# A new planner table and two changes of order in a hybrid decoder trunk whose token mixing runs beside an expert gather

## The reference

```
h = rmsnorm(x) @ w_in                      # u_a, v_a, val_b, gate_b, q_m and three gates, 1024 each
y_a = gelu(u_a) * (tril(w_s) @ layernorm(gelu(v_a)) + b)    # chunks of 128 tokens, 8 groups
y_b = silu(layernorm(causal_depthwise(val_b * sigmoid(gate_b), 31 taps)))
y_m = softmax(q_m k^T / 16) v              # 4 heads, 256 memory rows
x = x + (sig(g_a)*(y_a@w_o_a) + sig(g_b)*(y_b@w_o_b) + sig(g_m)*(y_m@w_o_m)) @ w_out
q = rmsnorm(x) @ w_q                       # 8 retrieval heads, product keys: two top-16 of 128,
                                           # then the top 16 of their 256 sums
x = x + sum over 8*16 experts of softmax(score) * gelu(xn . u_e) * v_e      # 16384 experts
```

## Time and profile before

| | |
|---|---|
| median of 3 runs | 2350.17 us (2345.11 to 2351.42) |
| profiled execution | 2351.42 us, its span 2348.7 us |
| PE, DVE, ACT, POOL busy | 69%, 67%, 28%, 29% |
| moved by DMA | 906 MB, of it 604 MB by POOL's gathers |

### The profile page before, as it was taken

The page is one execution under the profiler, slowest core; times in us unless marked ns, Lnnn a source line. Parts: engine busy times, 40 slices in busy tenths (PEclk is TensorE's granted clock), DMA queues, the critical chain, the costliest instruction groups (busy, mean ns, idle before and its releaser), DMA issues.

```text
span 2348.7 us, 32536 instructions
## 1 busy us (share of the span) xinstructions
PE 1625.2 (69%) x11468; PEld 1147.6 (49%) x11468; DVE 1584.5 (67%) x4217; ACT 666.4 (28%) x1654; POOL 677.7 (29%) x606
## 2 busy tenths in 40 slices
PE   8999848758898549777777635866899843333333
PEld 7899826527786217555666403743778610000000
DVE  2672258867766567898665556985966667776774
ACT  2112132521142323432131223342123233323221
POOL 0000032313233333232332232221422344444442
PEclk9999969968899759998899756986989965555555
DMA  7586699999899999999999999999989999999996
GB/s 278 178 303 238 249 386 401 418 421 388 355 419 420 420 409 422 421 421 422 421 420 420 421 418 382 394 421 408 370 354 421 420 421 421 418 422 411 417 408 272
DMA packets 127841, 905.98 MB, mean 386 GB/s; under 512 B 16112, under 2 KB 16576, under 8 KB 18368
## 3 DMA queue, kind: packets, MB, share of 16 engines
q0 software_dynamic: 82944, 604.02, 62.3%
q1 hardware_dynamic: 44736, 299.90, 32.2%
HBM read 895.75 MB, written 8.11 MB: 385 GB/s over the span
## 4 chain that ended last, share of the span: by engine, by line
PE 32%; DMA 31%; DVE 22%; ACT 4%; DVEq 4%; issue 4%; POOL 2%; POOLq 0%; SPq 0%; ACTq 0%
DMA uv<-uv_in,idx_u 24%; PE bank L1200 19%; DVE uv L1108 9%; DMA ring<-cache_in 5%; PE bank L1206 5%; PE bank L1574 4%; DVE yB L786 3%; POOL uv L405 2%; DMA ring<-w_in 2%; DVEq L781 1%; DVE x L1129 1%; ACT diag L731 1%; ACT L464 1%; DVE merged L794 1%; DVE yB L797 1%
## 5 line engine op out<-in xcount | busy, mean ns | idle before, releaser
L405 POOL DMA_INDIRECT uv<-uv_in,idx_u x576 | 635.5, 1103 | 1473.2 <-PE bank L1574 1066.8
L1108 DVE CUSTOM_DVE_ANT_0 uv<-uv,xrep 128x1024 f32<-128x1024 f32 x576 | 685.8, 1229 | 241.4 <-DMA uv<-uv_in,idx_u 240.9
L1574 PE MATMUL bank<-uv,diag 128*32 128x512 f32 x2304 | 431.1, 830 | 553.7 <-ACT diag L731 553.7
L1200 PEld LDWEIGHTS bank<-xnT,ring 128*128 128x128 f32 x4096 | 565.4, 206 | 105.1 <-issue 93.0
L1200 PE MATMUL bank<-xnT,ring 128*128 128x128 f32 (+1 forms) x4096 | 593.1, 307 | 6.8 <-DMA ring<-w_in 5.3
L1574 PEld LDWEIGHTS bank<-uv,diag 128*32 128x32 f32 x2304 | 55.2, 125 | 783.1 <-ACT diag L731 719.0
L464 ACT ACTIVATE pick<-pick 128x2 f32<-128x2 f32 (+1 forms) x324 | 69.6, 215 | 1128.9 <-DVE pick L1108 1128.3
L786 DVE SCALAR_TENSOR_TENSOR yB<-ext_p,small,yB 128x128 f32<-128x128 f32 x960 | 280.5, 354 | 20.4 <-issue 0.9
L464 ACT ACT_TABLE_LOAD x145 | 186.0, 1283 | 7.1 <-DMA x<-x_in 4.5
L731 ACT ACTIVATE diag<-gated_fold,pick 128x32 f32<-128x32 f32 x576 | 153.6, 314 | 9.7 <-ACT pick L464 0.3
L1200 PE MATMUL bank<-yMA,ring 128*128 128x128 f32 (+1 forms) x1024 | 136.7, 288 | 0.0
(11 more groups left out here) (161 smaller groups left out, 1481.4 us busy)
## 6 DMA issues: line engine op xcount, KB each, us to landing
ring<-w_in SPq DMA_DIRECT2D x224, 1024.0 KB, 9.8
ring<-cache_in SPq DMA_DIRECT2D x32, 1024.0 KB, 17.2
uv<-uv_in,idx_u POOLq DMA_INDIRECT x576, 17.2
phase<-rows_in SPq DMA_DIRECT2D x4, 1024.0 KB, 17.2
ring<-keys_in SPq DMA_DIRECT2D x4, 1024.0 KB, 10.1
ext_s<-state_in SPq DMA_DIRECT2D x2, 1088.0 KB, 10.4
convs_out<-ext_s SPq DMA_DIRECT2D x2, 1088.0 KB, 19.7
ext_s<-mem_in SPq DMA_DIRECT2D x2, 1024.0 KB, 18.5
```

What stands on the lines that cost most here:

```text
L405: nc.gpsimd.indirect_dma_start(out=uvbuf[2 * b + i], out_offset=None, in_=uv_in, in_offset=bass.IndirectOffsetOnAxis(ap=ids[:, c:c + 1], a ...
L1108: ins = V.tensor_tensor_reduce(out=u, in0=u, in1=xrep[gg % 2][:, :], scale=1.0, scalar=0.0, op0=ALU.mult, op1=ALU.add, accum_out=hid[:, c: ...
L1200: ins = MM(out, w[:, k, P * b:P * (b + 1)], rhs(k), start=k == 0, stop=k == KB - 1)
L1574: ins = MM(vbank[gg % 2][c:c + 32, :], diag[:, t % 4, i], uvbuf[2 * b + i][:, D + 512 * n:D + 512 * (n + 1)], start=first, stop=last)
```

## The change

It has four parts.

1. The planner's costs in `parts`: sk and sv 2 to 2.5; sg 1.5 to 2.5; csum and csq 2.5 to 3; tr2 9 to 12. `TAIL` 11 to 14.
2. The order of dense pieces: before, sg0, ua3, sg1, sg2, mg8, sg3, mg9; after, sg0, ua3, sg1, sg2, sg3, mg8, mg9. It holds in `parts` (and so in the turn of banks) and in PE's generator.
3. DVE's `gated`: the wait for projection and gate and the merge come before `conv(taps)`, not behind it, and the pieces 0, 8 and 16 start at the place of the next piece, not 2 units behind it.
4. For p = 1, ACT does `weigh(2)` (the exponential of head 2) behind `va(0)`, not ahead of it, and DVE does `att_norm(2)` ahead of `att_max(3)`.

```diff
-        out += some("sk", 2, 0, 1, 2) + O(3) + some("sk", 2, 3, 4, 5, 6, 7) + some("pts", 0.8, 0) + some("va", across, 3)
-        out += some("sv", 2, 0, 1) + some("pts", 0.8, 1) + some("sv", 2, 2, 3, 4, 5, 6, 7)
+        out += some("sk", 2.5, 0, 1, 2) + O(3) + some("sk", 2.5, 3, 4, 5, 6, 7) + some("pts", 0.8, 0) + some("va", across, 3)
+        out += some("sv", 2.5, 0, 1) + some("pts", 0.8, 1) + some("sv", 2.5, 2, 3, 4, 5, 6, 7)
...
-    out += some("mg", h, *range(2, 8)) + some("ua", h, 0, 1, 2) + some("sg", 1.5, 0)
-    out += some("ua", h, 3) + some("sg", 1.5, 1, 2) + some("mg", h / 2, 8) + some("sg", 1.5, 3) + some("mg", 3 * h / 2, 9) + [("csum", 2.5)] + some("mg", h, 10, 11, 12) + [("csq", 2.5)]
+    out += some("mg", h, *range(2, 8)) + some("ua", h, 0, 1, 2) + some("sg", 2.5, 0)
+    out += some("ua", h, 3) + some("sg", 2.5, 1, 2, 3) + some("mg", h, 8, 9) + [("csum", 3)] + some("mg", h, 10, 11, 12) + [("csq", 3)]
...
-    out += [("tr2", 9)] + some("wq", h, 0, 1) + some("sc", 1, 0) + some("wq", h, 2, 3) + some("sc", 1, *range(1, STEPS[p]))
+    out += [("tr2", 12)] + some("wq", h, 0, 1) + some("sc", 1, 0) + some("wq", h, 2, 3) + some("sc", 1, *range(1, STEPS[p]))
...
-LEAD, TAIL = 2, 11
+LEAD, TAIL = 2, 14
...
                     yield from turned(1)
-                    weigh(2)
                     yield place["S3"]
                     va(0)
+                    weigh(2)
...
+                    att_norm(2)
                     yield from att_max(3)
-                    att_norm(2)
...
-                        yield place[f"mg{c + 1}"] + 2 if c % 8 == 0 else place[f"mg{c}"]
-                        conv(taps)
+                        yield place[f"mg{c + 1 if c % 8 == 0 else c}"]
                         dve.wait_ge(S["pe_proj"], at("pe_proj", m, c + 1))
...
                             V.tensor_tensor(out, out, gate_c, ALU.add).then_inc(S["mg"], 1)
+                        conv(taps)
...
                 yield from spatial(2)
+                yield from spatial(3)
                 yield place["mg8"]
                 gate(8)
-                yield from spatial(3)
```

## The result

The change made the kernel slower: 2370.53 us (median of 4 runs, 2368.29 to 2372.66) against 2348.96 us for the kernel before beside it, a ratio of 1.0094 with a 95% interval of 1.0081 to 1.0107, or +22 us (+19 to +25). I had forecast 2341 us, range 2331 to 2354. The profiled execution after took 2376.01 us, its span is 2373.5 us, 24.8 us above the span before.

The account below looks back on a forecast made before the run. The prediction took the kernel to be bound by DMA bytes behind the start-up. From 2351.4 us it took 14.6 for two dry places, added 4.7 for a convolution, giving 2341.5, stated as 2341 us, range 2331 to 2354.

Parts of the forecast that it names:

- What bounds the kernel: Behind the start-up, DMA bytes at some 420 GB/s; the share falls short by 29.8 us, in few places.
- The pace and TAIL: More dense work beside each pair leaves PE less margin, 0.7 us instead of 1.0, but costs 0.
- the 13 us that I had called free: DMA's outstanding gathers last long enough that some 13 us between two `values` costs nothing, while 20 us does.
- my rivals: Dry places stay, 2351 (0.25); slower, 2359 (0.13); more than two places, 2333 (0.12); PE full, 2348 to 2351, counted with the first.
- Part 2 with the sg costs: At sg0 to mg9, p = 1: PE's long gap before sg3 goes, -14.6 us; the other end is 0.
- both dry places: Around sg3 in the two p = 1 mixings, 625 to 635 and 1725 to 1740 us: 7.6 and 7.0 us, both to go.
- Part 3: In DVE's gated pieces: piece 0's convolution loses idle time, +4.7 us; merges waiting for tanh cost 0.
- work in store: DMA's outstanding work hides tanh waits of merges in k = 3 and 5 pairs: 0, upper end 4.3 us.
- My slower rival: Merges wait 1.1 us in each of 8 gated pieces, 22 us with the convolution against -14.6: 2359 us; chance 0.13.
- POOL's multiplications: Layer norm of v, beside mg1 to mg4: as many DVE instructions stretched as before, 0, ends -2 and +2 us a portion.
- Part 4: With p = 1, DVE waits 3 us a portion for ACT's later exponential, hidden behind full DMA: 0, at most 6 us.
- The base of the sum: The terms were added to 2351.4 us, the profiled execution of the kernel before.

Follow-up runs that it names:

- e3: Kernel before with only the merge put ahead of the convolution and the 2 units of delay dropped: 2359.05 us, ratio 1.0048.
- e5: Kernel after with POOL's mask of the spatial weights moved earlier, from ua1's place to ua0's: 2351.43 us, 1.0015 of the kernel before.
- e7: Kernel before with only TAIL changed from 11 to 14: 2380.83 us, ratio 1.0130.
- e9: Kernel before with sg3 ahead of mg8 and sg costs of 2.5, POOL's mask at its old place: 2343.88 us, ratio 0.9980.
- e12: Kernel before with the merge ahead of the convolution, except pieces 0, 8 and 16, which stay as before: 2360.56 us, ratio 1.0048.
- e15: Kernel after with POOL's mask at ua0, the old convolution order, TAIL 11 and tr2 9: 2341.42 us, 0.9969 of the kernel before.
- e11: Kernel before with TAIL 14 and POOL's mask at ua0: 2359.35 us, ratio 1.0054.
- e10: Kernel after with POOL's mask at ua0 and the old order of convolution and merge: 2344.63 us, 0.9981 of the kernel before.
- e8: Kernel before with sg3 ahead of mg8, sg costs of 2.5 and POOL's mask at ua0: 2341.57 us, ratio 0.9968.
- e1: Kernel before with only sg3 put ahead of mg8, at the old costs: 2342.83 us, ratio 0.9973.
- e14: Kernel before with the merge ahead of the convolution only in pieces 1, 4, 6 and 7: 2363.09 us, ratio 1.0059.
- e4: Kernel before with only weigh(2) behind va(0) on ACT and att_norm(2) ahead of att_max(3) on DVE: 2348.46 us, ratio 1.0002.
- e2: Kernel before with only the new planner costs and TAIL 14, the old order of sg3 and mg8: 2362.32 us, ratio 1.0057.

## Why the prediction was wrong

**What bounds the kernel: right.** The shortfall of DMA is the measure, and it works better by bandwidth than by busy share. For windows of 5 us over 300 to 2300 us I added 5 x (1 - GB/s / 421):

| | before | after | e3 | e5 | e7 | e9 | e12 | e15 |
|---|---|---|---|---|---|---|---|---|
| shortfall, us | 51.1 | 74.2 | 61.2 | 52.6 | 82.9 | 42.3 | 64.1 | 40.2 |
| more than before | | +23.1 | +10.1 | +1.5 | +31.8 | -8.8 | +13.0 | -10.9 |
| span, more than before | | +24.8 | +10.8 | +1.4 | +32.1 | -8.3 | +13.3 | -10.6 |

By the share, which I used, the kernel after shows 13.7 us of its 24.8. The agreement by bandwidth is close to bookkeeping, since all kernels move the same bytes: it says that the lost time lies in this stretch and in which windows, not why.

**The pace and TAIL: the step that failed.** I took this term as 0 with -4 to +6 us. I laid out where PE meets its pieces, also that sg0 comes at pair 29, and asked each engine only for its time a pair. This is the overlap that I had wrong: I didn't ask what else sg0 waits for, nor where POOL is when PE gets there. The table put POOL's mask behind the gathers of the very pair that begins with sg0. The result shows 18.6 us for it (kernel after to e5) and again 17.8 us (e7 to e11). The gap of 16.2 us is above the 13 us that I had called free, so my own bound would have priced it, had I seen it. None of my rivals was this one. Step by step from the kernel after, the mask is 18.6 us (e5), part 3 is 8.0 (e10, predicted 4.7), and what is left stands at -4.5 (predicted -14.6).

**Part 2 with the sg costs: the mechanism right, the term too large.** -14.6 was predicted; e9 measured -4.7 and e8 -7.5, which their intervals don't tell apart. The wait of sg3 and both dry places went, and in e1, without the sg costs, the wait moved to mg8: for the dry places it takes both. In time e1 is as good (-6.3, overlapping intervals). What I missed is that the table also moves the pieces ahead: about 2.2 us are given back in the gated pieces and 3.9 us at 1040 to 1055.

**Part 3: too small, and the wrong half of it.** I had +4.7 for the convolution that loses DVE's idle time, and 0 for the merges that wait for the tanh. With the old table it is the other way round: e12 shows nothing for the first, e14 the whole 11 to 14 us for the second. I named pairs with k = 3 and 5 and "work in store"; in e12 four merges a portion wait, 7.3 us in the first. Together with POOL's multiplication (2.1 us) they make the dots late, and DMA comes up short at sg3. In the kernel after only pieces 6 and 7 wait, both in pair 27 (k = 3), 2.0 and 3.2 us in the two portions, 5.2 us against my upper end of 4.3. How the 8 us of e10 divide there was not tried. My slower rival had this mechanism (DVE's uncovered waits), but it priced it at 22 us, against 11 alone and 8 in e10. Beside the mask's wait most of it was hidden.

**POOL's multiplications.** I had 0 for the fact that both now fall into one pair. The convolution of 565.04 ended at 571.72, 0.7 us behind POOL's end, and one of its instructions took 2.54 us where the median is 0.35. "SBUF — State Buffer" of the Trainium skill, section "Who interferes with whom", calls the shared port pair an exclusive lock. By that rule, the trace agrees: POOL's two end at 568.63 and 571.05, and the two DVE instructions that met them (2.54 and 2.48 us long) ended at 568.80 and 571.20. In the p = 1 mixings no more DVE time is lost than before (8.1 us against 8.6 in the first), but 4.3 us of it are now lost between two `values`, which are 12.8 us apart there, and the window at 575 reads 0.44. So a gap of "some 13 us" isn't free everywhere. In portion 2 (p = 0), where POOL's two multiplications met nothing before, they now stretch two DVE instructions by 4.5 us together, which I had not looked at. What all this costs was not tried by itself.

**Part 4: right**, e4 measured 1.0002.

**The base of the sum.** I added to 2351.4, the profiled execution, which is the slowest of the four runs before. On their median, 2349.0, the same terms give 2339.

**What is left open:** the rest of the 12.7 us of e11 and the 17 us between e7 and e2, whether TAIL costs anything in the new order, and 2 us of later start of the first `values` (314.1 us after against 311.7 before, in one profile each).

## What to carry to other kernels

When a planner's table changes, make the map of pairs for every engine that takes part, the one that runs a pair behind too, and check each wait of the pieces that move: a piece that stands first behind the pair's own work has no cover. Work with slack, such as a mask of constants, belongs well ahead of its reader. Putting a consumer ahead of filler work is free only where its producer is done already or nearly; here the same exchange cost nothing in three pieces (2, 3 and 5) and 11 to 14 us in four. And the cost of a delay can show at the next dry place, not where the delay is.

## What the runs showed of the hardware

A wait of 4.7 us on PE cost 8.3 us between two `values`, since the work behind it ran at a granted clock of 0.50 (1.2 GHz) from 610 to 615 us, where e5, without the wait, reads 1.00: a piece of 32 matmuls took 6.20 instead of 4.61 us. The same chain, a wait of 4.26 us and then a gate of 4.45 instead of 2.44 us, stood between a wait of DVE of 1.10 us (piece 4) and one of 3.64 us (piece 7) in e12. Two POOL multiplications (2.35 and 2.33 us, 0.09 us apart) stretched one run of 8 DVE instructions from 2.35 to 6.68 us.
